# A joined set of edits to a hybrid decoder trunk: projection before the norm, array groups in the state-space stage, and expert results added into the residual rows in DRAM

## The chip, the cores and the metric

The kernel runs on one core of a Trainium2 chip. The metric is the device time of one execution in microseconds (us). Everything is float32. TensorE takes each f32 matmul in two passes, so the trace has two records for it; a transpose through TensorE has one.

## The reference

One layer of a decoder trunk on 1024 tokens of width 1024: an RMSNorm, one input projection whose columns feed a state-space head group and an attention head group, one output projection, and a mixture of experts (32 experts in 4 groups of 8; each token takes one group and two experts in it). A final RMSNorm ends it. Cut to its core:

```python
h = _rmsnorm(x, norm1_g); z = h @ w_in            # (1024, 1816)
y_ssm  = _s5_mixer(z[:, :512], ...)               # 32 channel groups of 16, 64 complex states each
y_attn = _nsa_mixer(...)                          # compressed, selected and window branches
x = x + concatenate([y_ssm, y_attn]) @ w_out
h = _rmsnorm(x, norm2_g)
g_val, g_idx = top_k(softmax(h @ rg_w + rg_b), 1)
e_val, e_idx = top_k(softmax(le[g_idx]), 2)       # two experts inside the group
for o in range(4):                                # coef is zero outside the chosen experts
    hid = silu(h @ w_gate[o]) * (h @ w_up[o])
    out = out + einsum('tef,efd->td', hid * coef[o][:, :, None], w_down[o])
return _rmsnorm(x + out, final_g)
```

## The kernel before

The stages run one after another, each in a block of its own with a barrier between; inside a stage the order on every engine is written out by hand and semaphores tie the engines together. P = 128 is a tile of tokens, NT = 8 the number of tiles, `psum[0..7]` are the eight PSUM banks.

**stage_project.** SP loads x (8 tiles of 512 KB), the constants (397 KB, after two tiles), and the columns of `w_in` for the queries as eight pieces of 64 columns. POOL loads the bias tables (311 KB) and then 16 small pieces of state-space parameters. ScalarE squares and sums each tile; VectorE turns the root into the inverse norm (`inverse_root`, L368 to L373, Newton steps); ScalarE and VectorE scale the tiles of x in turn; TensorE transposes each scaled tile (L304); VectorE copies the transposes into `ht` with the gain g1 (L357). Between the pairs TensorE makes five pieces of the bias rows (L291). Then come 40 jobs (L326, L329, L332), each a sum over 8 blocks of width 128 into one of four banks: 16 "f" jobs (features by 512 tokens), 16 narrow "t" jobs and 8 "t" jobs of 512 columns for the state-space input `u`. ScalarE empties all of them (L271 to L278); VectorE meanwhile works out the state-space parameters (`s5_parameters`).

**stage_s5.** TensorE transposes `u` (L653), makes the "taps" (L663: 16 groups, two parts each, 32 output columns by 128, all into PSUM partitions 0 to 31), which ScalarE copies (L629, four copies of 32 x 512), VectorE adds to (L748) and SP spreads into the zeroed `m3` by 16 loads (L588). Behind the taps TensorE transposes `m1t` (L653). The input product is L680; VectorE and POOL turn, scan (L765) and turn back (L732 to L778) in four parts; TensorE sums the output per bank from `own` (L690) and from the turned states (L704), first the four groups of one half of the state rows, then those of the other. ScalarE applies GELU (L638), and a gated product follows (L723).

**stage_out** projects, adds the residual into `x1` (SBUF), normalises, stores the normalised rows in DRAM (`xn_rows`, by SP) and makes the router's logits. **stage_route** works out, in one chain on VectorE, each token's two experts and coefficients, its slot in a list of 32 tiles of 128 slots (15 more are there for overflow), and by one-hot matmuls (L1470) the lists `dst` (2 token + choice) and `tok`.

**stage_experts.** For each of 32 tiles POOL gathers the rows from `xn_rows` (L1612), TensorE transposes them (L1631), multiplies with gate and up (L1637), transposes the hidden tile (L1644) and multiplies with down (L1655). ScalarE and VectorE each copy half of the result to `y` (two buffers), and POOL scatters it to `y_rows` (2048 rows, L1621), two rows a token. A buffer of `y` is written again only after its scatter has landed (`stored`). SP keeps four buffers of weights (3 MB each) filled (L1573, L1579).

**stage_final.** SP loads `y_rows` tile by tile (1024 KB each, three buffers); VectorE adds both rows times their coefficients to `x1` (L1915, L1916); ScalarE squares (L1887) and takes the root (L1889); VectorE makes the inverse; ScalarE scales (L1866), POOL multiplies with the final gain (L1906; the last tile on VectorE, L1927), and ScalarE's queue stores.

## Time and profile before

| | |
|---|---|
| median of 3 runs | 1248.17 us (1247.59 to 1250.56) |
| profiled execution, its own time | 1250.18 us |
| its span (first to last instruction) | 1248.3 us |
| PE busy | 1092.7 us, 88% |
| DVE, ACT, POOL busy | 506.9, 299.8, 190.0 us |
| expert loop, 838 to 1149 us | PE busy all the time |
| last scatter issued, first load of the last stage issued | 1186.1 us, 1195.1 us |
| input loads of the start | x 8 x 512 KB, constants 397 KB, tables 311 KB, w_in 8 x 256 KB |

Busy time is the time in which an engine executes; 1.9 us of the execution's time lie outside the span. PE is TensorE's matmuls, PEld its weight loads, DVE is VectorE, ACT ScalarE, POOL GpSimd, SP the queue of SyncE.

### The profile page before, as it was taken

What the parts mean: (1) busy time and instruction counts of PE and PEld (TensorE: products, weight loads), DVE (VectorE), ACT (ScalarE), POOL (GpSimd) and SP (SyncE); (2) the same over time, 40 slices, a digit from 0 to 9 for tenths busy, and PEclk for the clock granted to TensorE, in tenths of its full rate; (3) what the DMA queues carried; (4) which work ended last, traced back from release to release, by engine and by line L of the source; (5) the groups of instructions that cost most, each with busy time, mean ns of one, the idle gap of its engine ahead of it and who ended that gap; (6) DMA issues with size and microseconds to landing.
All of it is one profiled execution on the core that took longest, in us unless ns stands there. A gap on an engine that the chain in (4) does not pass through costs nothing. (4 is left out here: it accounts for less than half of the span.)

```text
span 1248.3 us, 13867 instructions
## 1 busy us (share of the span) xinstructions
PE 1092.7 (88%) x5123; PEld 650.8 (52%) x5123; DVE 506.9 (41%) x1173; ACT 299.8 (24%) x661; POOL 190.0 (15%) x233
## 2 busy tenths in 40 slices
PE   5999999858987799999999997399999999999900
PEld 3444787757436566666655554245445544545400
DVE  5199400395036576666632224612212221221157
ACT  5100110301013675665521001001011111101123
POOL 3000000161012321110110001011222122112124
PEclk9999999977998899999999999589999999999955
DMA  9110100132000640000002252349999999998064
GB/s 270 43 37 1 68 1 0 19 88 68 1 18 1 133 144 2 2 2 2 1 1 102 101 168 72 122 135 316 336 312 326 326 320 317 313 328 291 27 224 186
DMA packets 111544, 163.01 MB, mean 131 GB/s; under 512 B 26359, under 2 KB 94007, under 8 KB 106295
## 3 DMA queue, kind: packets, MB, share of 16 engines
q1 hardware_dynamic: 100224, 140.15, 34.7%
q0 software_dynamic: 10112, 17.92, 4.0%
q10 hardware_dynamic: 1152, 4.19, 0.8%
q8 instruction: 36, 0.59, 0.2%
q14 instruction: 20, 0.16, 0.0%
HBM read 152.58 MB, written 25.24 MB: 142 GB/s over the span
## 5 line engine op out<-in xcount | busy, mean ns | idle before, releaser
L1637 PE MATMUL banks<-shared,xt 128*128 128x512 f32 x512 | 227.4, 597 | 1.7 <-DVE xt L1676 1.7
L1637 PEld LDWEIGHTS banks<-shared,xt 128*128 128x128 f32 x512 | 95.9, 192 | 110.7 <-issue 110.7
L1655 PE MATMUL banks<-shared,hidt 128*128 128x512 f32 x256 | 115.2, 593 | 0.8 <-ACT hidt L1665 0.8
L1315 PE MATMUL banks<-wout,shared 128*128 128x512 f32 x256 | 112.7, 594 | 0.5 <-PEq L1051 0.5
L326 PE MATMUL banks<-x,wring 128*128 128x512 f32 x256 | 110.3, 592 | 0.0
L1681 DVE TENSOR_TENSOR hid_e<-act_g,banks 128x256 f32<-128x256 f32 x32 | 13.5, 421 | 220.0 <-ACT act_g L1661 220.0
L1099 ACT ACTIVATE shared<-shared,low 128x640 f32<-128x640 f32 (+7 forms) x128 | 92.9, 729 | 2.6 <-DVE low L1186 2.1
L1149 PE MATMUL banks<-consts,shared 128*128 128x128 f32 x528 | 78.8, 285 | 2.9 <-ACT shared L1099 2.1
L326 PEld LDWEIGHTS banks<-x,wring 128*128 128x128 f32 x256 | 48.5, 190 | 60.3 <-issue 60.3
L1149 PEld LDWEIGHTS banks<-consts,shared 128*128 128x128 f32 x528 | 56.7, 142 | 42.5 <-issue 37.4
L1315 PEld LDWEIGHTS banks<-wout,shared 128*128 128x128 f32 x256 | 47.6, 190 | 55.2 <-issue 55.2
L1131 PE MATMUL banks<-shared 64*128 64x512 f32 (+3 forms) x384 | 71.5, 489 | 1.5 <-PEq L824 0.9
L1655 PEld LDWEIGHTS banks<-shared,hidt 128*128 128x128 f32 x256 | 46.3, 191 | 47.3 <-issue 47.3
L1167 PE MATMUL banks<-shared 128*64 128x128 f32 x1056 | 68.7, 278 | 0.1
L1186 DVE CUSTOM_DVE_ANT_0 shared<-banks,bias 128x640 f32<-128x640 f32 (+4 forms) x96 | 52.7, 599 | 38.6 <-PE banks L1131 38.5
L1090 ACT COPY shared<-banks 128x512 f32<-128x512 f32 x88 | 46.8, 532 | 75.9 <-PE banks L1149 75.8
L1661 ACT ACTIVATE act_g<-banks 128x256 f32<-128x256 f32 x32 | 12.3, 384 | 209.3 <-PE banks L1637 209.3
L1167 PEld LDWEIGHTS banks<-shared 128*64 128x64 f32 x1056 | 57.0, 137 | 8.3 <-issue 8.1
L723 PE MATMUL banks<-shared,x 128*128 128x512 f32 x128 | 56.9, 607 | 3.1 <-DVE shared L785 3.1
L329 PE MATMUL banks<-wring,x 128*128 128x512 f32 x128 | 55.2, 593 | 0.0
L1687 DVE COPY y_e<-banks 128x512 f32<-128x512 f32 x32 | 22.1, 692 | 77.5 <-PE banks L1655 77.5
L1671 ACT COPY y_e<-banks 128x512 f32<-128x512 f32 x32 | 18.8, 586 | 126.9 <-PE banks L1655 126.9
(313 smaller groups left out, 1342.3 us busy)
## 6 DMA issues: line engine op xcount, KB each, us to landing
shared<-in_exp_w_down SPq DMA_DIRECT2D x32, 1024.0 KB, 5.0
shared<-in_exp_w_gate SPq DMA_DIRECT2D x32, 1024.0 KB, 9.0
shared<-in_exp_w_up SPq DMA_DIRECT2D x32, 1024.0 KB, 12.2
yt<-y_rows SPq DMA_DIRECT2D x8, 1024.0 KB, 6.2
shared<-in_x SPq DMA_DIRECT2D x8, 512.0 KB, 10.4
wring<-in_w_in SPq DMA_DIRECT2D x2, 2048.0 KB, 8.5
x<-in_x SPq DMA_DIRECT2D x1, 4096.0 KB, 31.6
xn_rows<-xn SPq DMA_DIRECT2D x8, 512.0 KB, 2.9
```

The lines of the kernel that those rows point to most:

```text
L326: ins = nc.tensor.matmul(bank[:], slot[:, c, n:n + P], ht[:, c, half * 512:half * 512 + 512], **flags)
L329: ins = nc.tensor.matmul(bank[:], tok, slot[:, c, :], **flags)
L723: ins = nc.tensor.matmul(psum[(2 + n % 2, 4 + n % 2)[part]][:], wglu[:, k, c0:c0 + P], yt[:, k, (n % 2) * 512:(n % 2) * 512 + 512], start= ...
L1090: copy(pt[u % 2][:, n0 * P:n0 * P + w], bank[:, 0:w]).then_inc(t_out[r % 2], 1)
L1099: nc.scalar.activation(prob[:, u % 2, at:at + n], prob[:, u % 2, at:at + n], ACT.Exp, bias=low[:, u % 2, v, j:j + 1], scale=-1.0, accum_ou ...
L1131: ins = nc.tensor.matmul(psum[2 * v + j][:, c0:c0 + k1 - k0], m["qt"][half, i, c * P:c * P + P], keys[half, k0:k1], start=True, stop=True)
L1149: ins = nc.tensor.transpose(psum[4 + r % 2][:, n * P:n * P + P], src, m["ident"])
L1167: ins = nc.tensor.matmul(psum[6 + br][half, i * P:i * P + P], vals[:, kb, half], pt[u % 2][:, at * P:at * P + P], start=n == 0, stop=n == ...
L1186: return V.tensor_tensor_reduce(out, scores, bias, 1.0, start, ALU.add, ALU.min, least)
L1315: ins = nc.tensor.matmul(psum[n % 4], src[:, i * P:i * P + P], m["wout"][:, k, half * 512:half * 512 + 512], start=k == 0, stop=k == KD - 1)
L1637: ins = nc.tensor.matmul(psum[2 + p], xt[:, p, k], wgu[:, b, k], start=k == 0, stop=k == KD - 1)
L1655: ins = nc.tensor.matmul(psum[6 + half], hidt[:, p, k], wd[:, b, k, half * 512:half * 512 + 512], start=k == 0, stop=k == 1)
```

## The change

**Start.** x is transposed as it is, four tiles, then the first job, then the rest between jobs 1 to 3. The scale is applied when a job is emptied: for the "f" jobs as a row over tokens (`scale`, made by TensorE from diagonal matrices, `scale_row`), for the token-major ones as a factor for each partition (`by_step` holds it in the order of `u`). VectorE now empties the "f" jobs and takes the parameters of the state space in pieces between them (`s5_parameters` is a generator). The bias rows come after jobs 4 to 8. SP loads x0, the constants and x1 to x3 first, then two pieces of `w_in` and one tile of x in turn; POOL's parameter loads wait until x2 and x3 are in. The order of the query jobs is first half of the tokens, then second.

```diff
+            sp.dma_start(x_tile[0], x_view[0]).then_inc(x_in[0], 16)
+            sp.dma_start(m["consts"][:], d["consts"]).then_inc(consts_in, 16)
+            sp.dma_start(g1[:], d["norm1_g"][0].rearrange("(p k) -> p k", k=KD)).then_inc(consts_in, 16)
+            for i in range(1, 4):
...
+            for n in range(4):
+                for v in range(KV):
+                    h, c0 = v * GQA + n, n * P + v * HD
+                    sp.dma_start(wring[:, 0, :, c0:c0 + HD], w_view[:, :, loads[0][0] + h * HD:loads[0][0] + h * HD + HD]
+                                 ).then_inc(w_loaded[0] if n > 1 else w_first[n], 16)
+                sp.dma_start(x_tile[4 + n], x_view[4 + n]).then_inc(x_in[2 + n // 2], 16)
...
+            gp.wait_ge(x_in[1], 32)
```

```diff
+            pe.wait_ge(consts_in, 32)
+            for i in range(4):
+                x_transposes(i)
+            pe.wait_ge(t_out, 8)
+            job(0)
+            scale_row(0)
+            x_transposes(4)
+            x_transposes(5)
+            job(1)
+            x_transposes(6)
+            x_transposes(7)
+            job(2)
+            scale_row(1)
+            raw_parameters()
+            job(3)
+            pe.wait_ge(t_out, 16)
+            for k in range(4, len(jobs)):
+                job(k)
+                if k < 9:
+                    bias_row(k - 4)
+                if k in (5, 7):
+                    by_steps(k // 2 - 2)
+
```

```diff
+            def scaled(k):
+                kind, load, n, half, dst = jobs[k]
+                if load:
+                    dve.wait_ge(rows_stored, 16)
+                else:
+                    dve.wait_ge(scale_out, half + 1)
+                dve.wait_ge(mm_done, k + 1)
+                negated = (load, n) in ((1, 2 * P), (2, 0))
+                V.scalar_tensor_tensor(dst, psum[4 + k % 4], HD ** -0.5 if load == 0 else -1.0 if negated else 1.0,
+                                       scale[:, half * 512:half * 512 + 512], ALU.mult, ALU.mult).then_inc(f_out, 1)
...
+            for i in range(4):
+                transposed(i)
+            inverses(0)
+            transposed(4)
+            transposed(5)
+            scaled(0)
+            transposed(6)
+            transposed(7)
+            inverses(1)
+            parts = s5_parameters(nc, dve, chain, m, s5, bri, cri, tmp, psum, s5_in, raw_t, exp_in, exp_out)
+            next(parts, None)
+            for k in range(1, len(jobs)):
+                if jobs[k][0] == "f":
+                    scaled(k)
+                    for _ in range(2):
+                        next(parts, None)
+            for _ in parts:
+                pass
```

**State space.** The taps of four groups go to four groups of 32 array columns in turn (PSUM partitions 0, 32, 64, 96), and ScalarE copies each by itself (16 copies of 32 x 128). The turned states' product alternates between the two halves of the array's rows.

```diff
-                nc.scalar.copy(taps[:, 4 * n:4 * n + 4], psum[4 + n][0:both].rearrange("p (g c) -> p g c", g=4)
-                               ).then_inc(taps_out, 1)
+                for k in range(4):
+                    ins = nc.scalar.copy(taps[:, 4 * n + k], psum[4 + n][k * both:k * both + both, 0:P])
+                ins.then_inc(taps_out, 1)
...
             for n in range(4):
-                for k in range(4):
-                    gl = 4 * n + k
-                    for ri in range(2):
-                        ins = nc.tensor.matmul(psum[4 + n][0:both, k * P:k * P + P],
+                for ri in range(2):
+                    for k in range(4):
+                        gl = 4 * n + k
+                        ins = nc.tensor.matmul(psum[4 + n][k * both:k * both + both, 0:P],
                                                bbz[:, ri, gl].rearrange("p v h -> p (v h)"),
                                                m["m2"][:, ri, gl, 0:STEPS * GH], start=ri == 0, stop=ri == 1)
...
-                if n == 4:
+            for n in range(4):
+                if n == 2:
                     pe.wait_ge(products, 16)
                     for later in range(4, 8):
                         own(later)
-                pe.wait_ge(turned, n // 2 + 1)
-                half = slice((n % 2) * 64, (n % 2) * 64 + 64)
+                pe.wait_ge(turned, n + 1)
                 for k in range(4):
-                    gl = 4 * (n // 2) + k
+                    gl = 4 * n + k
                     for ri in range(2):
-                        ins = nc.tensor.matmul(psum[n][:, k * P:k * P + P], s[half, gl, ri], m["m2"][half, ri, gl, GH:],
-                                               start=False, stop=k == 3 and ri == 1)
-                ins.then_inc(y_done, 1)
+                        for gh in range(2):
+                            half = slice(gh * 64, gh * 64 + 64)
+                            ins = nc.tensor.matmul(psum[2 * n + gh][:, k * P:k * P + P], s[half, gl, ri],
+                                                   m["m2"][half, ri, gl, GH:], start=False, stop=k == 3 and ri == 1)
```

**Output stage and routing.** SP also stores x1 to new rows `x_rows` in DRAM. The lists are the token of each slot and, by one matmul of twice the columns, its coefficient (`slot_coef`). `place` puts expert e of group g at slot tile 4 e + g, so that the tiles that follow each other belong to four different groups; the loads of weights follow that order.

```diff
+                sp.wait_ge(x_done, 2 * i + 2)
+                sp.dma_start(x_rows[i], m["x1"][:, i]).then_inc(m["x_stored"], 16)
...
+                ins = nc.tensor.matmul(psum[2][:, 0:2 * tiles], row_hot[:, n], tile_hot[:, n].rearrange("p w t -> p (w t)"),
                                        start=n == 0, stop=n == 2 * NT - 1)
...
-            chain.note(V.tensor_scalar(ch["val"][:, 0], m["pair"], -float(DUMMY), None, ALU.add))
-            ts(ch["val"][:, 1], m["pair"], 1.0 - DUMMY, ALU.add)
+            ts(ch["val"][:], bc(m["token"], 2, 1), -float(DUMMY), ALU.add)
             for k in range(2):
                 dve.wait_ge(m["xn_stored"][k], 16 * NT // 2)
-            tt(tile_hot[:], bc(c["eid"], tiles, 2), bc(m["row"][:, 0:tiles], 2 * NT, 1), ALU.is_equal)
-            tt(tile_hot[:], tile_hot[:], bc(c["val"], tiles, 2), ALU.mult)
+            hot = tile_hot[:, :, 1]
+            tt(hot, bc(c["eid"], tiles, 2), bc(m["row"][:, 0:tiles], 2 * NT, 1), ALU.is_equal)
+            tt(tile_hot[:, :, 0], hot, bc(c["val"], tiles, 2), ALU.mult)
+            for k in range(2):
+                tt(hot[:, k * NT:k * NT + NT], hot[:, k * NT:k * NT + NT], bc(m["coef"][:, :, k], tiles, 2), ALU.mult)
...
-            chain(V.tensor_copy(m["dst"], list_f[:]))
-            ts(m["tok"], m["dst"], 1, ALU.arith_shift_right)
-
-
-UN = 4
+            chain(V.tensor_copy(m["tok"], list_f[:]))
+            chain(V.tensor_copy(m["slot_coef"], psum[2][:, tiles:2 * tiles]))
+            m["chained"] = chain.n
```

**Experts and end.** The coefficient multiplies the hidden tile, and the scatter adds to `x_rows` instead of writing to `y_rows`. The last stage loads the 8 tiles of `x_rows` (512 KB each), squares and normalises them in pairs, and multiplies on VectorE alone.

```diff
         gp.wait_ge(s["y_act"], n + 1)
-        nc.gpsimd.tensor_copy(dst[:, p:p + 1], m["dst"][:, bass.ds(col, 1)]).then_inc(s["dst"], 1)
+        gp.sem_inc(s["let_go"], 1)
+        nc.gpsimd.tensor_copy(dst[:, p:p + 1], m["tok"][:, bass.ds(col, 1)]).then_inc(s["dst"], 1)
         gp.wait_ge(s["dst"], n + 1)
         gp.wait_ge(s["y_dve"], n + 1)
         gp.sem_inc(s["let_go"], 1)
-        nc.gpsimd.indirect_dma_start(m["y_rows"], bass.IndirectOffsetOnAxis(dst[:, p:p + 1], 0), y[:, p], None,
-                                     bounds_check=limits[1], oob_is_err=False).then_inc(stored[p], 16)
+        nc.gpsimd.indirect_dma_start(m["x_rows"], bass.IndirectOffsetOnAxis(dst[:, p:p + 1], 0), y[:, p], None,
+                                     bounds_check=limits[0], oob_is_err=False, compute_op=ALU.add).then_inc(stored[p], 16)
...
         dve.wait_ge(s["act"], n + 1)
-        V.tensor_tensor(hid[:, p], act_g[:, p], psum[2 + p][:, DE:2 * DE], ALU.mult).then_inc(s["hid"], 1)
+        V.scalar_tensor_tensor(hid[:, p], act_g[:, p], m["slot_coef"][:, bass.ds(n, 1)], psum[2 + p][:, DE:2 * DE], ALU.mult, ALU.mult
+                               ).then_inc(s["hid"], 1)
...
+                sp.dma_start(m["x1"][:, i], rows[i]).then_inc(x_in[i], 16)
+            for i in range(NT):
+                sp.wait_ge(o_done, i + 1)
+                sp.dma_start(out_rows[i], m["x1"][:, i]).then_inc(stored, 16)
+            sp.wait_ge(stored, 16 * NT)
...
+            nc.scalar.activation(root[:, 0:1], m["eps"], ACT.Sqrt)
+            for q in range(NT // 2):
+                for i in (2 * q, 2 * q + 1):
+                    act.wait_ge(x_in[i], 16)
+                    nc.scalar.activation(junk[:, i % 2], m["x1"][:, i], ACT.Square, accum_out=ss[:, i:i + 1]).then_inc(ss_done, 1)
+                act.wait_ge(ss_done, 2 * q + 2)
+                nc.scalar.activation(root[:, 2 * q:2 * q + 2], ss[:, 2 * q:2 * q + 2], ACT.Sqrt, bias=m["eps"], scale=1.0 / D
                                      ).then_inc(root_done, 1)
...
+            chain = Chain(dve, chain_s, m["chained"])
+            for q in range(NT // 2):
+                pair = slice(2 * q, 2 * q + 2)
+                dve.wait_ge(root_done, q + 1)
+                inverse_root(nc, chain, rstd[:, pair], root[:, pair], ss[:, pair], newton)
+                for i in (2 * q, 2 * q + 1):
+                    x = m["x1"][:, i]
+                    V.scalar_tensor_tensor(x, x, rstd[:, i:i + 1], m["fg"][:], ALU.mult, ALU.mult).then_inc(o_done, 1)
```

All stages also share one semaphore for VectorE's chains of dependent operations.

## Rows read from the trace of the kernel before

**Rows 1.** Windows of four stages: engines' busy time (records), clock, DMA share, GB/s
```profile
...
15.00:32.40 17.40, 16.49 (x78) 11.28 (x78) 14.42 (x38) 12.80 (x22) 0.54 (x1) 1.00 1.16 274
838.00:1149.00 311.00, 311.00 (x927) 154.72 (x926) 63.11 (x109) 34.44 (x83) 66.87 (x110) 1.00 0.93 320
1149.00:1184.50 35.50, 34.65 (x97) 16.43 (x95) 5.78 (x11) 3.77 (x10) 4.90 (x9) 1.00 0.15 54
1195.00:1248.30 53.30, 0.00 (x0) 0.00 (x0) 39.82 (x65) 20.32 (x32) 19.06 (x7) 0.50 0.63 236
```

**Rows 2.** Timeline of the start: start us, us, engine, line; last, the projection's end
```profile
...
5.95 20.05 SPq L200 DMA_DIRECT2D wring<-in_w_in  x8
...
15.16 3.65 PE L304 MATMUL banks<-consts,shared 128*128 128x128 f32 x16 [5.08 <-DVE shared L346]
...
25.06 2.05 PE L304 MATMUL banks<-consts,shared 128*128 128x128 f32 x16
...
27.05 0.98 PE L291 MATMUL banks<-shared 33*8 33x484 f32 x2
...
32.44 38.03 PE L326 MATMUL banks<-x,wring 128*128 128x512 f32 x88
...
217.55 10.89 PE L329 MATMUL banks<-wring,x 128*128 128x512 f32 x25
```

**Rows 3.** Timeline of the state-space stage, 228 to 299 us
```profile
...
235.94 7.17 PE L663 MATMUL banks<-m,w 128*32 128x128 f32 x64
...
243.15 0.57 ACT L629 COPY s<-banks 32x512 f32<-32x512 f32 x1 [1.17 <-PE banks L663]
...
247.59 6.46 PE L680 MATMUL banks<-shared,x 128*64 128x128 f32 x112 [0.83 <-ACT x L576]
...
279.69 6.50 PE L704 MATMUL banks<-m,s 64*128 64x128 f32 x32 [5.59 <-DVE s L778]
...
286.12 5.92 PE L690 MATMUL banks<-x,shared 128*128 128x128 f32 x32
...
291.48 0.69 DVE L778 TENSOR_TENSOR s<-w,shared 128x508 f32<-128x508 f32 x1
...
291.98 6.39 PE L704 MATMUL banks<-m,s 64*128 64x128 f32 x64
```

**Rows 4.** Timeline of routing, 795 to 806 us
```profile
...
796.53 0.94 DVE L1479 TENSOR_TENSOR tile_hot<-tile_hot,c_val 128x752 f32<-128x752 f32 x1
...
798.25 7.06 PE L1470 MATMUL banks<-tile_hot,row_hot 128*128 128x47 f32 x32 [11.73 <-DVE row_hot L1552]
```

**Rows 5.** Expert loop: its timeline, the scatter's line, the software DMA queue (830 to 1187 us)
```profile
...
838.57 0.38 ACT L1665 COPY hidt<-banks 128x256 f32<-128x256 f32 x1
...
839.81 1.02 POOL L1621 DMA_INDIRECT y_rows<-y_e,dst_s  x1 [0.89 <-POOL dst_s L1617]
...
851.20 1.01 POOL L1621 DMA_INDIRECT y_rows<-y_e,dst_s  x1 [0.86 <-POOL dst_s L1617]
...
DMA to landing us min/median/max: 3.2/7.2/8.5
...
q0 software_dynamic: 8496, 15.29, 11.3%
```

**Rows 6.** The chain that ended last, in order of time: start us, us, what
```profile
...
1195.08 4.77 DMA yt<-y_rows
...
1202.51 1.15 ACT junk L1887 x2
...
1204.97 0.30 ACT root L1889
...
1206.33 0.02 DVEq L1924
...
1219.09 3.27 DVE x L1916
...
1243.77 1.29 DVE o L1927
```

More of the change, by code:

```diff
@@ L188, in stage_project @@
+    for load, firsts, toks in ((1, ("kct", "vct", "kst"), NT), (2, ("kwt",), NT), (3, (), STEPS)):
+        jobs += [("f", load, n * P, half, m[name][:, half * 512:half * 512 + 512]) for n, name in enumerate(firsts)
+                 for half in range(2)]
+        jobs += [("t", load, i, 0, None) for i in range(toks)]
     last_of_load = [max(k for k, job in enumerate(jobs) if job[1] == load) for load in range(4)]
+    count = {kind: [sum(job[0] == kind for job in jobs[:k + 1]) for k in range(len(jobs))] for kind in "ft"}
@@ new lines, in bias_row, with by_steps @@
+                nc.tensor.matmul(psum[2][0:HEADS, 0:w], tabx, tables[:, c0:c0 + w], start=True, stop=True
+                                 ).then_inc(rows_done, 1)
+            def by_steps(h):
+                pe.wait_ge(scale_out, 2)
+                if h:
+                    pe.wait_ge(step_out, 1)
+                for j in range(4):
+                    src = scale.rearrange("p (c j) -> p j c", j=STEPS)[:, 4 * h + j]
+                    ins = nc.tensor.transpose(psum[3][:, j * P:j * P + P], src, m["ident"])
+                ins.then_inc(step_done, 1)
@@ L320, in _, with job @@
+            def job(k):
+                kind, load, n, half, dst = jobs[k]
+                bank, slot = psum[4 + k % 4], wring[:, load % 2]
+                if k < 2:
+                    pe.wait_ge(w_first[k], 32)
+                elif k == 2:
+                    pe.wait_ge(w_loaded[0], 16 * w_dmas[0])
+                if load and jobs[k - 1][1] != load:
                     pe.wait_ge(w_loaded[load % 2], 16 * w_dmas[load])
                 if k >= 4:
-                    pe.wait_ge(mm_out, k - 3)
+                    before = jobs[k - 4][0]
+                    pe.wait_ge(f_out if before == "f" else tok_out, count[before][k - 4])
@@ L325, in _ @@
                     if kind == "f":
-                        ins = nc.tensor.matmul(bank[:], slot[:, c, n:n + P], ht[:, c, half * 512:half * 512 + 512], **flags)
+                        c0 = n * P if load == 0 else n
+                        ins = nc.tensor.matmul(bank[:], slot[:, c, c0:c0 + P], ht[:, c, half * 512:half * 512 + 512], **flags)
                     elif load == 3:
@@ new lines, in inverses @@
+            def inverses(h):
+                four = slice(4 * h, 4 * h + 4)
+                dve.wait_ge(root_done, h + 1)
+                inverse_root(nc, chain, rstd[:, four], root[:, four], ss[:, four], newton)
+                dve.sem_inc(inverse_done, 1)
+                if h:
+                    dve.wait_ge(scale_done, h)
+                for i in range(4):
+                    V.tensor_scalar(diag[:, i], m["ident"], rstd[:, 4 * h + i:4 * h + i + 1], None, ALU.mult).then_inc(diag_ready, 1)
@@ new lines, in scaled @@
+            def scaled(k):
+                kind, load, n, half, dst = jobs[k]
+                if load:
+                    dve.wait_ge(rows_stored, 16)
+                else:
+                    dve.wait_ge(scale_out, half + 1)
[3 more added lines that the diff above has]
+                                       scale[:, half * 512:half * 512 + 512], ALU.mult, ALU.mult).then_inc(f_out, 1)
```

354 lines of the change are left out of this document (158 added, 196 removed).

## The prediction

> **What bounds the kernel now.** I read the windows of the stages first [rows 1]. In the expert loop (838 to 1149 us) TensorE is busy for all 311 us while the 16 DMA engines are busy for 0.93 of it at 320 GB/s: TensorE sets the pace, and the DMA engines are a close second. In the last stage (1195 us to the end) TensorE does nothing; VectorE is busy for 39.8 of 53.3 us. In the first 32.4 us TensorE runs but does no projection yet. So the edits can only gain where TensorE waits or does preparatory work: at the start, in the state-space stage, in routing, and in the last stage. Then I read the timeline of the start [rows 2], of the state-space stage [rows 3], of routing [rows 4], the scatters [rows 5], and last the chain that ended the run [rows 6]: it begins with the load of y_rows at 1195.1 us and then stays almost wholly on VectorE, alternating with waits for nothing else.
>
> **The start (projection before the norm is known).** Before, x is scaled by its inverse norm, then transposed; projection starts at 32.44 us and then runs without a gap, one f32 matmul record of 512 columns each 0.436 us (10.89 / 25), 16 of them or 6.9 us for a full job [rows 2]. After, x is transposed as it lands, the first projection job (first half of the tokens) needs only four tiles, and the scale comes in at the eviction. But TensorE is the bound from there on, so what counts is work, not order. First job: the loads x0, constants, x1, x2, x3 and the tables (2.8 MB) at the 320 GB/s of [rows 1] take about 9 us after the first microsecond or two, so x3 is there near 11 us. Four transposed tiles cost 1.83 us each at the slow rate that the rows at 15.16 us show (3.65 for two tiles), so from about 8.5 us they end near 16, and the first job starts near 16.5. The w_in columns for it (two issues of about 2.5 us each, 20.05 / 8) come right behind x3, near 13 us: hidden. What TensorE then has to do between jobs, and had behind it before: four tiles of transposes 4.1 (2.05 for two at the fast rate), five bias rows at 0.98 = 4.9, two broadcast matmuls of the scale with 512 columns in two passes each, 4 x 0.436 = 1.7, eight transposes for the scale by step 1.0, the raw parameters 0.9: 12.6 us. The slow rate still applies until 24 us in the rows; if it lasts one or two microseconds into the first job, that costs 1. So 16.5 + 12.6 + 1 = 30.1 in place of 32.4: I take **-2**. Ends: -5 (transposes at the fast rate, x earlier) and +3 (first job wholly slow, 6.9 us lost). VectorE takes the evictions of 16 jobs and the parameters of the state space in turn; a job is 6.9 us and there are four banks, so a VectorE step of a few us is hidden. If the cover were gone, TensorE would wait for the step. POOL's 16 small loads now stand behind the wait for x0 to x3, are issued over some 11 us, and land near 29 us; TensorE needs them after the third job, near 41 us. x7 comes behind all w_in columns of the first load, near 28 us; it is wanted near 33.
>
> **State space, column and row groups.** The taps (64 records of 32 output columns) take 7.17 us, 112 ns each, one group after the other; L680, whose matmuls alternate between two column halves, takes 58 ns (6.46 / 112) [rows 3]. So alternating groups do run side by side. With four groups in turn the taps take 64 x 58 = 3.7 us or less. Now ScalarE decides: 16 copies of 32 x 128 in place of four of 0.57. A copy of 256 columns takes 0.38 [rows 5] and one of 512 takes 0.57, so 128 columns are about 0.28, and 16 are 4.5 us. They begin 0.9 us after the taps, 236.8, and end at 241.3 instead of 243.7. The copies behind them in ScalarE's queue, the first products on VectorE and the m3 loads by SP all move up by **2.4**.
> The Trainium skill, "TensorEngine Tiling (Array Packing)", Theoretical Speedup, gives up to 4x for 32 columns, and its section PSUM Bottleneck says that tiling does not speed up emptying PSUM. By the 4x the taps would take 1.8 us and ScalarE's copies would still end at the same time, so the sum stays.
> At the tail, the L704 matmuls took 6.50 us for 32 at the slow rate and 6.39 for 64 at the fast one. After, row halves alternate: 3.3 us for the second group, which lets the later L690 matmuls (5.92) start 3.2 earlier, so they are done before VectorE's last product. That product (292.17 now, 289.8 after) then releases 32 records instead of 64 being left: at 50 ns 1.6 us, at 100 ns 3.2. The end moves from 298.4 to between 291.4 and 293.0, and two last activations instead of one follow (0.6). Total for the stage, with the 2.4 in it: **-5.5**. Ends: -7.5, and +1 if groups do not overlap (16 copies are then the only change, +0.6, and two activations).
>
> **Output projection and routing.** SP issues eight more stores of 0.5 MB, each ahead of the wait for xn; an issue is a third of a microsecond, and the wait for xn comes later anyway; x_done precedes it. Nothing there sets TensorE's time. If a store were late, the wait for xn_rows in routing would see it, 22 us later. Routing is one chain on VectorE: the product on tile_hot stays (0.94 for 752 elements) and two of half its size (about 0.55) are added: +1.1, one constant operation less. The 32 matmul records of L1470 take 0.22 each with 47 columns; with 94 columns they may take the same, if weights bound them, or at most 47 more columns at 1.7 ns (twice 0.436 / 512, the clock is at its lower level there), +2.6. I take **+1.5**, ends +0.9 and +4.
>
> **Expert loop and scatters.** The order of experts alters addresses, not bytes or waits. The scatter becomes an accumulating one. Before: POOL 1.02 us per issue, landing 7.2 us median, 8.5 at most [rows 5]. Gather and scatter together are 11.3% of 16 engines' time over 357 us, so the scatters are half, 20 us. No row shows an accumulating transfer. Below: the same price as a plain one, 0. If each row moves twice (read, then write), 20 us more over 311 take the share from 0.93 to 0.99: still under TensorE, cost 0. I take **0** here, and **+1** for the last scatter's landing, which lies on the path (3.2 us for the last one; ends 0 and +4). The product with slot_coef is on VectorE, busy for 63 of 311 us [rows 1].
> A rule against the change: the Trainium skill, "DMA: Bandwidth & Descriptors", Rules for kernel authors, states that an accumulating DMA reads its destination and writes it later. By it alone the extra time would be the 0.06 of share above.
>
> **Last stage.** Before, 53.2 us from 1195.08 to 1248.3 [rows 6]: per tile two VectorE products, the second of up to 3.27 when POOL multiplies beside it where a like one alone takes 1.29, and the Newton steps. After: eight loads of 0.5 MB. At 320 GB/s a tile takes 1.64; the first is there after about 3.2 and the second at 4.8. Square 1.05 and read 0.2, root 0.3 (table already loaded): 6.4. Then VectorE per pair: Newton 1.06, two products of 1.29 = 3.65; four pairs 14.6: 21.0. Last load 14.7 + 1.6 = 16.3, before 17.4 when VectorE wants it. Last store 1248.3 - 1245.1 = 3.2: 24.2. Gain **-29.0**. Ends: -31 (loads at over 400 GB/s), and -23 if 8.4 MB of loads and stores share 320 GB/s and the last store comes at 27 + 3.2.
>
> **Sum**: -2 - 5.5 + 1.5 + 0 + 1 - 29 = -34 against the profiled execution's own 1250.2: 1216.2. The median of the runs is 2.0 lower: **1214.2**.
>
> **Rivals.**
> (A) The accumulate makes the DMA engines the bound. Free are 0.07 x 311 = 22 us, and some 20 us more, since the weights are all in 36 us before TensorE ends and the last tile needs about 16 of them. So up to 42 us more are hidden: a scatter may cost 3.1 times a plain one. At four times 60 - 42 = 18 us are lost: 1232. For it: the share of 0.93. Against it: a mere reread costs 20.
> (B) The groups do not overlap and the first job is wholly slow: +6.5 and +5, 1225. Against it: L680.
> (C) Slower than before: the landing time of an accumulating scatter holds the y buffers. A buffer is written again two tiles after (2 x 11.39 us), the scatter is issued 1.7 us after, so 21.1 us of landing are free. Beyond it each us costs half a us in some 30 tiles, 15 us. At 23.4 us, 3.2 times today's median, all 34 us are gone; at 24, 1214 + 44 = 1258. Against it: 8.5 is today's largest.
> (D) The change in the last stage does little, as loads and stores fight: 1220.
>
> **Chances.** Forecast 0.62, D 0.10, B 0.10, A 0.13, C 0.05. Of A a small part reaches no gain. Range 1206 to 1232: it leaves out the upper part of A, and C. Faster by over 0.3% (3.7 us, what a measurement of this kernel can tell): 0.95; same 0.01; slower 0.04.
>
> **What would show it.** The first L326-like record near 16.5 us and the stage's end near 226; taps under 4 us; the turned-back matmuls at 50 to 60 ns per record; one period of the loop still 11.4 us with a DMA share near 0.99; scatter landing under 21 us; the last stage 24 us long with products of 1.29 us and POOL idle. Wrong it would be if the expert period exceeds 11.5 us, if TensorE or ScalarE waits for a stored semaphore, or if the last stage waits for loads.

## The result, and the profile after

The changed kernel takes 1217.56 us at the median (1214.97 to 1218.44, 4 runs), the kernel before 1248.07 (1247.59 to 1250.56, 4 runs): ratio 0.9748, 95% interval 0.9728 to 0.9768. Forecast were 1214.2 us, within 1206 to 1232. The profiled execution has a span of 1215.1 us against 1248.3, 33.2 less.

First the windows of the stages after: the start up to the first projection job, the expert loop over the same stretch as in [rows 1], its last 28 us, and the last stage.

```profile
core 0: us, PE busy (x) PEld busy (x) DVE busy (x) ACT busy (x) POOL busy (x), PEclk, DMA share, GB/s
7.00:23.40 16.40, 13.38 (x49) 9.39 (x50) 7.68 (x18) 8.14 (x14) 9.66 (x16) 1.00 1.15 275
838.00:1149.00 311.00, 310.31 (x923) 154.30 (x922) 64.59 (x109) 33.57 (x81) 82.09 (x108) 1.00 0.95 305
1149.00:1177.20 28.20, 27.16 (x73) 12.58 (x71) 4.25 (x8) 3.36 (x9) 5.29 (x6) 1.00 0.50 131
1190.70:1215.10 24.40, 0.00 (x0) 0.00 (x0) 13.30 (x32) 11.75 (x22) 0.00 (x0) 0.50 0.89 344
```

TensorE is still busy all through the loop, short of 0.7 us, though the DMA engines now carry the adding scatters; near the end they stay half busy (0.50) where their share had been 0.15 [rows 1]. The last stage is 24.4 us long.

TensorE's timeline of the start (L301 are the transposes of x, L356 and L308 the projection jobs and the broadcast of the scale), to be set beside [rows 2].

```profile
9.08 6.40 PE L301 MATMUL banks<-consts,shared 128*128 128x128 f32 x32 [9.08 <-DMA shared<-in_x]
16.42 7.13 PE L356 MATMUL banks<-x,wring 128*128 128x512 f32 x16 [0.94 <-DVE x L397]
23.39 1.02 PE L308 MATMUL banks<-shared,consts 128*128 128x512 f32 x2
24.25 2.10 PE L301 MATMUL banks<-consts,shared 128*128 128x128 f32 x16
26.19 7.03 PE L356 MATMUL banks<-x,wring 128*128 128x512 f32 x16
```

The first job starts at 16.42 us (forecast 16.5) and takes 7.13: it isn't slow, so the 1 us set aside for that came back. The state-space stage starts at 226.3 us in place of 229.4.

The timeline of that stage: L770 and L736 are the taps and their copies, L787 the input product, L797 the product `own`, L812 the turned-back matmuls, to be set beside [rows 3].

```profile
232.86 1.95 PE L770 MATMUL banks<-m,w 128*32 128x128 f32 x64
233.57 4.32 ACT L736 COPY s<-banks 32x128 f32<-32x128 f32 x16 [0.46 <-PE banks L770]
242.19 8.54 PE L787 MATMUL banks<-shared,x 128*64 128x128 f32 x112 [0.83 <-issue]
...
279.37 4.55 PE L797 MATMUL banks<-x,shared 128*128 128x128 f32 x32
285.66 2.06 PE L812 MATMUL banks<-m,s 64*128 64x128 f32 x32 [1.74 <-DVE s L887]
288.24 2.06 PE L812 MATMUL banks<-m,s 64*128 64x128 f32 x32 [0.52 <-DVE s L887]
```

A tap takes 30 ns where it took 112, so four column groups do run side by side; ScalarE's 16 copies (4.32 us, estimated at 4.5) are now the longer part, and TensorE, after 16 transposes, stands idle for 1.84 us behind them. L787 then runs for a while at the lower granted clock (0.50 from 242 to 246 us, 1.2 GHz), 8.54 us for 112 records in place of 6.46. At the tail a turned-back record takes 64 ns, inside the 50 to 100 of the forecast.

The scatters' line (issue times in ns; the last line is from issue to landing), against [rows 5]:

```profile
L1737 POOL DMA_INDIRECT x_rows<-y_e,dst_s x32: 1563/1595/1624, 831.2 to 1178.9; - x32
DMA to landing us min/median/max: 5.9/9.3/10.8
```

An issue takes POOL 1.60 us in place of 1.02, and a landing 9.3 us at the median in place of 7.2. Landing stays far under the 21 us at which rival C would begin.

Position against the kernel before, in the two profiled executions: state-space stage begins 3.1 us earlier; its gated projection (L832) 7.6; routing 9.1; first expert matmul 8.0; last scatter's issue 7.2; first load of the last stage 4.3; end 33.2.

### The profile page after: what moved, and what is told of

It is laid out like the page before. It is cut to its first block and busy times, and to the rows that moved or that the text cites. A ratio compares the mean times of both kernels' runs of the same rounds, so it can differ in the third digit from the quotient of the medians.

```text
span 1215.1 us, 13911 instructions
## 1 busy us (share of the span) xinstructions
PE 1078.8 (89%) x5135; PEld 636.1 (52%) x5135; DVE 491.6 (40%) x1149; ACT 283.1 (23%) x645; POOL 190.1 (16%) x226
## 5 line engine op out<-in xcount | busy, mean ns | idle before, releaser
L1753 PE MATMUL banks<-shared,xt 128*128 128x512 f32 x512 | 226.8, 596 | 2.6 <-DVE xt L1792 1.7
L356 PE MATMUL banks<-x,wring 128*128 128x512 f32 x256 | 112.0, 594 | 0.9 <-DVE x L397 0.9
L1797 DVE SCALAR_TENSOR_TENSOR hid_e<-act_g,slot_coef,banks 128x256 f32<-128x256 f32 x32 | 15.4, 481 | 222.9 <-ACT act_g L1777 222.9
L356 PEld LDWEIGHTS banks<-x,wring 128*128 128x128 f32 x256 | 47.9, 190 | 60.0 <-issue 58.0
L1428 PEld LDWEIGHTS banks<-wout,shared 128*128 128x128 f32 x256 | 47.6, 190 | 55.2 <-issue 55.2
L832 PE MATMUL banks<-shared,x 128*128 128x512 f32 x128 | 57.6, 613 | 3.1 <-DVE shared L894 3.1
L1737 POOL DMA_INDIRECT x_rows<-y_e,dst_s x32 | 51.0, 1594 | 27.0 <-POOL dst_s L1733 27.0
L359 PE MATMUL banks<-wring,x 128*128 128x512 f32 x128 | 55.2, 593 | 0.0
## 6 DMA issues: line engine op xcount, KB each, us to landing
shared<-in_exp_w_up SPq DMA_DIRECT2D x32, 1024.0 KB, 17.6
```

Of the source, the lines that this page charges most:

```text
L356: ins = nc.tensor.matmul(bank[:], slot[:, c, c0:c0 + P], ht[:, c, half * 512:half * 512 + 512], **flags)
L359: ins = nc.tensor.matmul(bank[:], tok, slot[:, c, :], **flags)
L832: ins = nc.tensor.matmul(psum[(2 + n % 2, 4 + n % 2)[part]][:], wglu[:, k, c0:c0 + P], yt[:, k, (n % 2) * 512:(n % 2) * 512 + 512], start= ...
L1428: ins = nc.tensor.matmul(psum[n % 4], src[:, i * P:i * P + P], m["wout"][:, k, half * 512:half * 512 + 512], start=k == 0, stop=k == KD - 1)
L1737: nc.gpsimd.indirect_dma_start(m["x_rows"], bass.IndirectOffsetOnAxis(dst[:, p:p + 1], 0), y[:, p], None, bounds_check=limits[0], oob_is_e ...
L1753: ins = nc.tensor.matmul(psum[2 + p], xt[:, p, k], wgu[:, b, k], start=k == 0, stop=k == KD - 1)
```

## The experiments

Three groups, each on one chip with its own runs of the kernel before. I compare ratios to that kernel; 0.001 is 1.25 us. The unaltered changed kernel ran in the second group.

**1. The changed kernel again.**

> The changed kernel itself, unaltered, so that the kernels run beside it and the earlier ones have a ratio to set theirs against. Both theories: a ratio of 0.974 to 0.976 to the kernel before.

Measured: ratio 0.9739, interval 0.9726 to 0.9753. Its state-space stage starts at 225.9 us and L832 at 298.7, 72.8 us later, where the first execution had 73.6 and the kernel before 78.1: here L787 took 6.46 us, and the stretch at the lower clock lay in the taps (3.48 us instead of 1.95), where ScalarE's copies hide most of it. The traces of the later runs that leave this stage as it is put it between 72.2 and 75.0 us, so up to 3 us of it depend on where the clock falls in an execution.

**2. A scatter that doesn't add.**

```diff
-bounds_check=limits[0], oob_is_err=False, compute_op=ALU.add
+bounds_check=limits[0], oob_is_err=False
```

> The changed kernel with a scatter that overwrites instead of adding, so x_rows loses x and one of the two expert rows of each token (the output is not the reference's); all counts of instructions and bytes written stay. Theory 1 (each adding scatter reads its destination too): POOL's issue falls from 1.60 to about 1.0 us, the scatter lands in about 7.2 us instead of 9.3 at the median, the DMA share of the loop falls from 0.99 to about 0.94, TensorE's waits for weights near 1138 and 1150 us go away (1.5 us), and the last scatter lands about 2.9 us earlier after its issue: 1217.6 - 1.5 - 2.9 = 1213.2 us. Rival (landing and waits come from the shape of the transfer or from the weights' addresses, not from adding): the time stays at 1217 to 1218.

Measured: ratio 0.9689 (0.9675 to 0.9702), 6.2 us faster than the changed kernel; 4.4 were expected. The trace agrees with theory 1 in each place: issue 1.01 us, median landing 7.6 us instead of 9.3 (the second line below, in us), no wait of TensorE for weights, and from the last scatter's issue (1177.83) to the first load of the last stage (1186.80) 9.0 us instead of 11.8. The loop (1.4 us) and this (2.8) make the 4.2 us that the edit explains; the last stage is also 1.0 us shorter in this trace, but over the traces that leave it as it is it varies from 23.4 to 25.2 us.

```profile
L1737 POOL DMA_INDIRECT x_rows<-y_e,dst_s x32: 977/1011/1017, 831.5 to 1177.8; - x32
x_rows<-y_e,dst_s POOLq DMA_INDIRECT x32, 7.6
```

**3. A second scatter, plain or adding, and two plain ones.** The output stage also fills a spare array, and each scatter is followed by one into it; the counts of the semaphore that frees y are doubled.

```diff
+nc.gpsimd.indirect_dma_start(m["spare"], bass.IndirectOffsetOnAxis(dst[:, p:p + 1], 0), y[:, p], None,
+                             bounds_check=limits[0], oob_is_err=False).then_inc(stored[p], 16)
```

> The changed kernel, in which each scatter is followed by a second one of the same rows, not adding, to a spare array of the same size (and the output stage fills that array too, 4 MB more). It adds 32 times 0.5 MB. Theory 1 (the loop has 0.01 of its DMA time free, and the weights were done some 25 to 36 us before the loop's end): the 20 us of 16 engines' time that a plain scatter costs over the loop are hidden but for a few us, 1218 to 1224 us. Rival (a share of 0.99 means no room at all): +20 us, 1238.

> As the kernel with a second plain scatter, but the second scatter adds as well. It adds some 42 us of 16 engines' time (the software queue took 0.179 of 350 us against 0.113 of 357 before, so an adding scatter costs about 2.1 plain ones). Theory 1: about 22 us are still hidden at the loop's end, so 1217.6 + 20 = 1238 us, with TensorE waiting for weights from the first third of the loop on. Rival A of the prediction had the free time at 42 us beside a plain scatter, of which 22 are used up: the same 1238. Rival (DMA engines overlap the read with other work, so the share overstates the cost): 1218 to 1225.

> The kernel with a second plain scatter, in which the first one does not add either, so that x_rows loses x and one expert's row (the output is not the reference's). Theory 1 (an adding scatter cost 40 us of the DMA engines' time more than a plain one over the loop, as the second adding against the second plain scatter showed, a plain one 34, and the loop has 38 to 40 us free beside one plain scatter): the 34 are hidden: as with one plain scatter, 1212 to 1215 us. Rival 1 (the free time is 22 us and an extra read costs 20, as the shares say): 12 us are lost, 1224. Rival 2 (nothing is free beside the plain one): 1212 + 34 = 1246.

Ratios: a second plain one 1.0022 (1.0013 to 1.0031); a second adding one 1.0337 (1.0321 to 1.0353); two plain ones and none adding 0.9737 (0.9712 to 0.9761). The expected 1218 to 1224 and 1238 us for the first two were wrong by 30 and 55 us (1253.3 and 1293.4 measured), and both rivals (1238, and 1218 to 1225) were too low as well. From the waits of each trace, the lines in which TensorE's matmuls wait for weights (total us, times, longest), first with a second plain scatter:

```profile
PE banks L1757 <- DMA shared<-in_exp_w_up: 25.8, 14, 3.2
```

With a second adding one:

```profile
PE banks L1757 <- DMA shared<-in_exp_w_up: 50.4, 21, 6.4
```

With two plain ones:

```profile
PE banks L1757 <- DMA shared<-in_exp_w_up: 0.9, 2, 0.7
```

The loop's length, from its first gate matmul to its last down matmul, in each trace, with the time in it in which TensorE's matmuls are busy, and the granted clock:

| scatters of each expert | loop, us | TensorE busy, us | clock | software queue's share of DMA time, 830 to 1180 us (830 to 1215 and 1250 where two ran long) |
|---|---|---|---|---|
| one plain | 368.1 | 366.4 | 1.00 | 11.6% |
| one adding (the change) | 369.5, again 369.3 | 366.9 | 1.00 | 17.9% |
| two plain | 371.1 | 368.5 | 0.99 | 17.6% |
| one adding, one plain | 404.2 | 376.8 | 0.98 | 22.6% |
| two adding | 443.1 | 391.0 | 0.94 | 25.5% |

Adding in place of plain is worth 443.1 - 404.2 = 38.9 us where next to nothing is hidden, and a plain scatter 404.2 - 369.5 = 34.7: an adding one costs 74 us over the loop, 2.1 plain ones. Part of both sums is TensorE's own time, since the granted clock is lower where it waits: its 1080 records are busy 9.8 us longer with the plain scatter added, and another 14.2 when that one adds as well. Counted by TensorE's idle time alone a plain scatter costs 24.9 us and the adding another 24.7, so an adding scatter costs 2.0 plain ones. Whether the loop would have kept the same length at the full clock wasn't tried, so the prices lie between 25 and 39 us; the factor of 2 holds either way.

With a single scatter, adding in place of plain took only 1.4 us (369.5 against 368.1), so 24 to 37 us were free beside one plain scatter, by the one count or the other. Two plain ones lose 3.0 us against one, 2.1 of them TensorE's busy time at a lower clock and 0.9 idle time, so a second plain scatter is hidden too. Rivals 1 and 2 of that run foresaw 12 and 34 us lost and fall. Its theory (1212 to 1215) was too low: the ratio puts the kernel 6.0 us above the one with a plain scatter, near 1218 us. In the traces 3.0 of that lie in the loop and 4.0 at its end, where 13.0 us instead of 9.0 pass from the last scatter into `x_rows` to the first load, which waits for the landing of the second scatter as well.

The share of busy DMA time doesn't show the limit. The window from 900 to 1000 us, first in the changed kernel, then with a second plain and with a second adding scatter:

```profile
900.00:1000.00 100.00, 100.00 (x299) 49.78 (x298) 20.66 (x35) 10.33 (x25) 26.91 (x35) 1.00 0.96 308
900.00:1000.00 100.00, 94.09 (x269) 46.20 (x268) 18.97 (x32) 9.97 (x24) 30.91 (x40) 0.97 0.92 299
900.00:1000.00 100.00, 84.77 (x236) 41.49 (x236) 16.58 (x28) 8.67 (x21) 32.37 (x35) 0.91 0.90 274
```

Where TensorE waits for weights the share is 0.92 and 0.90, not higher but lower. From 838 to 1149 us it is 0.92 and 0.89 in these two runs, and between 0.92 and 0.96 in those that wait little or not at all. So a share of 0.93 doesn't mean that 7% of the time is free.

**4. The experts in order, each scatter behind the landing of the one before.**

```diff
-"place": np.broadcast_to(UN * (np.arange(E) % EPG) + np.arange(E) // EPG, (P, E)),
+"place": np.broadcast_to(np.arange(E), (P, E)),
-load_gate_up(nc, d, m, sp, EPG * u + i, u)
+load_gate_up(nc, d, m, sp, n, u)
...
+if landed is not None:
+    gp.wait_ge(stored[1 - p], landed)
```

> The changed kernel with the experts in the reference's order (slot n is expert n) and with a wait on POOL, ahead of each scatter, for the landing of the scatter before it. Theory 1 (a scatter lands 5.9 to 10.8 us after its issue and the period is 11.4 us, so the wait is over when POOL comes to it): 1217.6 us, within 2. Rival (POOL stands at the wait, the gather behind it is issued late, and TensorE misses its rows): each period loses 1 us or more, 1230 to 1250 us, with TensorE waiting for xg.

Measured: ratio 0.9764 (0.9749 to 0.9779), 3.1 us slower than the changed kernel, with intervals that just overlap; theory 1 had it within 2. The line of the waits that says where:

```profile
POOL x_rows L1739 <- DMA x_rows<-y_e,dst_s: 3.0, 1, 3.0
```

In the loop POOL never waits, as theory 1 has it: a period is longer than a landing. It waits once, for 3.0 us, at the last scatter, which comes soon after the one before it (1174.27 and 1178.93 us in the changed kernel, 4.7 apart). Theory 1 had missed that. The loop itself was 373.1 us long, 3.6 more than in the changed kernel: 2.4 of it is TensorE's busy time at a lower clock near the loop's start, 1.2 idle time. Whether the order of the weights' addresses has a part in this was not separated.

**5. Each of the early edits undone: the start, the taps, the row halves.** The first puts the projection stage of the kernel before in the changed kernel. The second:

```diff
-for ri in range(2):
-    for k in range(4):
-        ins = nc.tensor.matmul(psum[4 + n][k * both:k * both + both, 0:P], ...
+for k in range(4):
+    for ri in range(2):
+        ins = nc.tensor.matmul(psum[4 + n][0:both, k * P:k * P + P], ...
```

and four copies of 32 x 512 with it. The third restores the loop over eight banks with one row half each.

> The changed kernel with the projection stage of the kernel before (x scaled by its inverse norm, then transposed; first projection job near 32 us). The traces have the state-space stage's first TensorE instruction at 226.3 after and 229.4 before. Theory 1: the whole 3.1 us is given back, 3.1 us slower than the changed kernel. Rival (the start's gain is partly paid again in the state-space stage, whose clock and queue positions then differ): 1 to 2 us slower.

> The changed kernel with the taps of the kernel before (64 matmuls into the same 32 rows, one after the other, and four copies of 32 x 512 on ScalarE). Theory 1: the taps take 7.2 us instead of 1.95, the copies behind them end at 240.3 instead of 237.9, and the first product on VectorE and all behind it, which VectorE bounds, is late by 2.4 to 3.0: 2.4 to 3 us slower. Rival (the 1.6 us that the first matmuls of the next step lost at the slow clock, 8.5 against 6.5 us, go away again, since TensorE is not idle before them): 1 us slower or less.

> The changed kernel with the turned-back matmuls of the kernel before (all 32 of one row half, then all 32 of the other). Theory 1 (at the tail 64 records at 100 ns, 6.4 us, take the place of two groups of 32 at 64 ns, and the other 32 before VectorE's last product): 3 us slower. Rival (VectorE's last product sets the end and only the last group counts): 6.4 - 2.1 = 4.3 us slower, less 0.6 for one activation fewer behind it.

Ratios: old start 0.9772 (0.9758 to 0.9787), old taps 0.9763 (0.9748 to 0.9777), old halves 0.9772 (0.9752 to 0.9791): 4.1, 3.0 and 4.1 us slower than the changed kernel, each uncertain by about 2. With the old start the state-space stage begins at 229.5 instead of 225.9 us (3.6; in the other traces with the new start it begins between 224.8 and 226.8), and nothing of it is paid again: the stage is 73.4 us long, between the 72.8 and 73.6 of the two traces of the changed kernel. With the old taps the timeline shows 7.92 us of them:

```profile
232.85 7.92 PE L769 MATMUL banks<-m,w 128*32 128x128 f32 x64
240.81 0.57 ACT L735 COPY s<-banks 32x512 f32<-32x512 f32 x1 [1.17 <-PE banks L769]
241.49 0.41 DVE L856 TENSOR_TENSOR s<-s,s5b_tmp 32x256 f32<-32x256 f32 x1 [7.21 <-ACT s L735]
```

Counted from the stage's start (225.4 us here), the copies end after 16.0 us instead of 11.6 and 12.1 in the changed kernel, the first product comes after 21.0 instead of 17.9 and 16.9, and L831 starts after 76.3 instead of 73.6 and 72.8: 2.7 to 3.5, as theory 1 has it. But 1.6 us of that come from the clock, which was at its lower level for a part of this stretch (0.70 from 232 to 236 us): the 12 transposes ahead of the taps took 2.39 us instead of 1.53, and the taps 7.92 instead of 7.17. Without this 1.1 to 1.9 are left, between theory 1 and its rival. In the kernel before, where nothing ran slow there, the first product comes after 19.4 us, so the new taps are worth 1.5 and 2.4 us in the two traces. With the old halves the last group is the one row of 64:

```profile
285.35 6.39 PE L811 MATMUL banks<-m,s 64*128 64x128 f32 x64
```

The next matmuls begin at 292.43. From the stage's first product on VectorE to the gated projection 58.2 us pass instead of 55.7 and 55.8 (55.2 to 56.2 in all traces with the new halves, 58.7 in the kernel before): 2.5 more. That is nearer to theory 1 (3) than to its rival (3.7), but the time (4.1, uncertain by 2) does not separate them.

**6. The last stage: bytes, or the product on POOL.**

```diff
 for i in range(NT):
+    sp.dma_start(more[:, i], more_rows[i]).then_inc(x_in[i], 16)
     sp.dma_start(m["x1"][:, i], rows[i]).then_inc(x_in[i], 16)
```

> The changed kernel, whose last stage loads 4 MB more (rows of xn_rows into a spare buffer, one tile of them ahead of each tile of x_rows; the square of a tile waits for both), as many bytes as the last stage of the kernel before read. Theory (the last stage is set by bytes, at the 336 to 394 GB/s that its windows show): 4.2 MB more are 11 to 12 us, 1229. Rival (VectorE's 3.45 us for each pair sets it, as the prediction has it, and the loads are behind it): 5 us or less.

Measured: ratio 0.9817 (0.9792 to 0.9842), 9.8 us slower than the changed kernel; in the trace the last stage is 33.7 us long, 9.3 more. The theory had 11 to 12, the rival 5 or less. The windows of the whole stage and of its middle:

```profile
1192.70:1226.40 33.70, 0.00 (x0) 0.00 (x0) 13.47 (x32) 11.86 (x22) 0.00 (x0) 0.50 0.94 373
1200.00:1224.00 24.00, 0.00 (x0) 0.00 (x0) 13.47 (x32) 9.23 (x18) 0.00 (x0) 0.50 1.03 415
```

With the DMA engines full the traffic runs at 415 GB/s, and 4.2 MB at that are 10.1 us. So the changed last stage has next to no DMA time to spare, about 1 us (10.1 - 9.3). In the changed kernel itself VectorE still sets the end: from its first instruction of the stage (1196.98 us) to its last (1211.12) it is idle for 0.15 us, and the last pair's root is ready 1.3 us before VectorE takes it.

For the kernel before, the product of all eight tiles in one VectorE instruction:

```diff
-nc.gpsimd.tensor_tensor(o[:, i % 2], m["x1"][:, i], m["fg"][:], ALU.mult).then_inc(o_done, 1)
+V.scalar_tensor_tensor(o[:, i % 2], m["x1"][:, i], rstd[:, i:i + 1], m["fg"][:], ALU.mult, ALU.mult
+                       ).then_inc(o_done, 1)
```

> The kernel before, in whose last stage VectorE does the product with the inverse norm and the final weights in one instruction for all eight tiles, as it did for the last one alone; POOL and ScalarE's product go. VectorE then has 3 products of 1.28 us and 1.1 us of Newton steps for each tile, 4.9 us, 39 us in all. Theory (VectorE's second product at 3.3 us and a slow Newton step, both beside a product on POOL, made the last stage long): 1199.9 + 39 + 3.2 = 1242 against a span of 1248.3, 6 us faster, a ratio of 0.995. Rival (loads and their buffers set the pace): no change.

Measured: ratio 0.9995 (0.9982 to 1.0008): the rival. The stage is 53.0 us long as before. The costliest groups of that stage:

```profile
L1899 DVE SCALAR_TENSOR_TENSOR x<-yt,coef,x 128x1024 f32<-128x1024 f32 x8 | 10.3, 1285 | 0.3
L1909 DVE SCALAR_TENSOR_TENSOR o<-x,rstd,fg 128x1024 f32<-128x1024 f32 x8 | 10.3, 1284 | 6.8 <-DMA out<-o 6.7
```

The second product takes 1285 ns on average where it took 2046, as the theory said, so a product on POOL beside it does slow it. But VectorE then waits 6.7 us for the two output buffers, whose stores ScalarE issues late, and the stage is as long as it was. Without that wait it would come near the expected time; this was not tried.

**7. Two waits less.** Two of each bank's four tap copies go to VectorE, and the last scatter's indices are copied ahead of the wait for its rows.

```diff
-for k in range(4):
+for k in range(2):
     ins = nc.scalar.copy(taps[:, 4 * n + k], psum[4 + n][k * both:k * both + both, 0:P])
...
+for k in range(2, 4):
+    ins = V.tensor_copy(taps[:, 4 * n + k], psum[4 + n][k * both:k * both + both, 0:P])
...
-scatter(gp, E - 1, 1, E - 1)
+nc.gpsimd.tensor_copy(dst[:, 1:2], m["tok"][:, E - 1:E]).then_inc(s["dst"], 1)
+gp.wait_ge(s["y_dve"], E)
+nc.gpsimd.indirect_dma_start(m["x_rows"], ..., compute_op=ALU.add)
```

> The changed kernel with two small edits that the traces point to. (1) Two of the four taps' copies of each bank go to VectorE, which stands idle for 3.7 us there: ScalarE's 16 copies of 4.3 us become 8, the first product on VectorE comes about 2 us earlier. (2) The row indices of the last scatter are copied on POOL before the last expert's rows are ready, not after (0.9 us of idle time ahead of every scatter's issue). Theory: 2 + 0.9 = 2.9 us faster than the changed kernel, a ratio of 0.9716. Rival (the m3 loads or the clock set the next step, and the last scatter is issued no earlier because VectorE's copy comes last): 0 to 1 us.

Measured: ratio 0.9714 (0.9693 to 0.9735), 3.1 us under the changed kernel's 0.9739 and close to the expected 0.9716, but on another chip and with overlapping intervals: it beats the kernel before, and is likely, not shown, to beat the changed one. The trace gives each edit its size. The first product comes 15.9 us after the stage's start instead of 17.9 and 16.9, and L832 72.0 instead of 73.6 and 72.8: 0.7 to 1.6 us. The last scatter is issued 1.47 us after VectorE begins the copy of its rows, instead of 1.74: 0.3 us, since most of the pause ahead of the issue stays without the index copy. Together these are 1.0 to 1.9 us and not the 2.9 expected, so the agreement of the ratio is in part luck.

## Why the forecast was right, step by step

| step | forecast | measured |
|---|---|---|
| start | -2 | -3.1, undone 3.6 in the trace |
| state space | -5.5 | -4.5, again -5.3 |
| up to routing's start | 0 | -1.5 |
| routing | +1.5 | +1.1 |
| expert loop | 0 | +0.8 |
| last scatter's landing | +1 | +2.9 |
| last stage | -29.0 | -28.8 |
| sum | -34 | -33.1 |

**Start.** Right, and the reserve of 1 us for a slow first job was not needed (it took 7.13 us; 6.9 was the forecast at full clock). From the first job to TensorE's last matmul of the stage 12.9 us more pass than before; the forecast had 12.6.

**State space.** Both mechanisms hold. The taps take 1.95 us and not 3.7, which changes nothing, since ScalarE's copies decide, as forecast. The Trainium skill, "TensorEngine Tiling (Array Packing)", Theoretical Speedup, has up to 4x for 32 columns; this trace shows 112 / 30 = 3.7. By part, the first product came 1.5 and 2.4 us earlier after the stage's start in the two traces (forecast 2.4), and the rest of the stage was 3.1 and 2.9 us shorter (forecast 3.1). What was missing is the stretch at the lower clock. It lies in L787 (8.5 to 8.6 us) in the five traces in which the copies leave TensorE a pause of 1.84 to 1.86 us, and in the taps or the transposes ahead of them in the others. Whether the pause causes it is not shown: with the old taps, and with half of the copies on VectorE, there is no such pause, and the stretch is there all the same, ahead of or in the taps.

**Up to routing, and routing.** In the second trace of the changed kernel the way from L832 to the first expert matmul is 507.5 us, as long as before; in the first it is 507.2. The -1.5 and the +1.1 are thus sure only together, to about 1 us. The list matmuls of 94 columns took 7.14 us against 7.06 for 47 [rows 4]: twice the columns cost nothing, and the 2.6 us at the far end were not due.

**Expert loop.** The 0 was right, its working was not. The step "if each row moves twice, 20 us more over 311 take the share from 0.93 to 0.99: still under TensorE" read the price off the queue's share of DMA time. By the share, adding did cost 22 us (17.9% against 11.6% of 350). By the pace it is 38.9 (24.7 by TensorE's idle time alone), and a plain scatter 34.7 (24.9) and not 20. The free time, worked out as 42 us, was 24 to 37. So where the forecast left 22 us unused, next to nothing was left: a further plain scatter made the loop 34.7 us longer, and in the changed kernel TensorE already waits four times for weights, 2.2 us in all, and with one plain scatter each never. Rival A put the edge at 3.1 times a plain scatter's price; it lies at 1.9 to 2.1 (a plain scatter's price and the free time, over that price), and the adding scatter stands on it. That the term came out at 0 was therefore luck in part. The windows' share gave no warning: 0.95 over 838 to 1149 us, at 305 GB/s, less than the 0.99 forecast, and the two loops that do lose time have 0.92 and 0.89 there. The step "free are 0.07 x 311" took a share of 1.00 for full, and these runs are full below it. On the rule that I weighed there, the Trainium skill, "DMA: Bandwidth & Descriptors", Rules for kernel authors (an adding transfer reads its destination and writes it later): the factor of 2 agrees with it.

**Last landing.** The term was mis-sized: +2.9, not +1. Between the last scatter's issue and the first load lie 11.8 us instead of 9.0, and 9.0 again when the scatter doesn't add. It is the one place where the price of adding lies wholly on the path.

**Last stage.** 24.4 us, 24.2 forecast, and by the forecast's own terms: 6.3 us to VectorE's first step (6.4), 14.1 for its chain (14.6), 4.0 to the end of the last store (3.2). Two readings behind it were incomplete. That POOL slowed VectorE holds for single instructions, but its removal alone gains nothing: without POOL the old stage stays at 53.0, with waits for the output buffers in its place. And the new stage has only about 1 us of transfers to spare: with the bytes that the old one loads it takes 33.7. So 9.3 of the 28.8 us would be lost again with 4.2 MB more; what these bytes cost in the old stage, and how the gain divides among them and the chain of adding, square, root, product and store through two output buffers, was not tried.

**The rivals.** B falls (groups overlap, first job at speed); C falls (10.8 us at most, 21 free); D falls (24.4 us); A falls for this change, though with next to nothing to spare and not with 22 us.

## What to carry to other kernels

Price a transfer by what a second one of its kind costs where nothing is hidden, not by its queue's share: here the share said 20 us where the pace said 35 and 39, or 25 if only TensorE's idle time is counted. A term forecast as "hidden" wants its cover measured too, since 0 with 22 us to spare and 0 on the edge look the same in the total. An instruction that contention makes twice as long is no bound until a kernel without the contention is faster; here it was not.

## What the runs showed of the hardware that I had not expected

- An adding scatter of 128 rows of 4 KB takes POOL 1.60 us to issue, a plain one 1.01, and costs the loop twice as much (74 against 35 us for 32 of them by the loop's length, 50 against 25 by TensorE's idle time). The software queue's share grew only from 11.6% to 17.9%, and the weights beside it landed later: medians 11.8, 19.0 and 15.4 us for gate, up and down instead of 9.0, 12.4 and 5.0. Two plain scatters do the same to them (11.3, 19.2 and 15.6).
- The mean DMA share doesn't tell a full loop: from 838 to 1149 us it is 0.92 and 0.89 where TensorE waits for weights over and over, and 0.92 with one plain scatter, where it never does.
- Four 32-column groups of f32 matmuls ran at 30 ns a record, two 64-row groups at 64 ns, against 112 and about 100 for the same shapes one after the other.
- Loads and stores of contiguous rows ran at 415 GB/s with the DMA engines full, above the 320 GB/s on which the forecast had built.
